# A fused fp32 transformer kernel on one core: the order of the thirty-four input-projection units is permuted

## The chip, the cores and the metric

The kernel runs on one core of a Trainium2 chip. The metric is the device time of one execution in microseconds (us); lower is better. The engines are called as the profile calls them: PE (TensorE, matmuls), DVE (VectorE), ACT (ScalarE), POOL (GpSimd), and SP, which here only issues transfers. Each runs its own list of instructions in order and waits on semaphores that the others raise.

## The reference

Two transformer blocks run one after the other on 512 tokens of width 1024, in fp32. What matters here is the middle of the first block:

```python
u = rmsnorm(h, mix_norm[l])
(fq, fk, fv, ff, dq, dk, dv, iq, ik, iw, mq, g) = jnp.split(u @ w_in[l], SPLIT_POINTS, axis=-1)
fq = rmsnorm(fq.reshape(B, S, FOX_HEADS, FOX_HEAD_DIM), fox_q_norm[l])      # fk alike
dq = rope(rmsnorm(dq.reshape(B, S, DSA_HEADS, DSA_HEAD_DIM), dsa_q_norm[l]), cos, sin)   # dk alike
iq = rope(iq.reshape(B, S, IDX_HEADS, IDX_DIM), cos_i, sin_i)               # ik alike
km, vm = jnp.split(rmsnorm(mem, mem_norm[l]) @ w_mem_kv[l], 2, axis=-1)
km = rmsnorm(km.reshape(B, M, MEM_HEADS, MEM_HEAD_DIM), mem_k_norm[l])
mq = rmsnorm(mq.reshape(B, S, MEM_HEADS, MEM_HEAD_DIM), mem_q_norm[l])
```

Before it stands a SwiGLU feed-forward layer. After it come three attentions (forget-gated "fox", top-k "dsa" whose keys an indexer picks, and one over 256 memory tokens), gates, an output projection, a second feed-forward layer, and then the second block.

## The kernel before

Activations lie transposed, with 128 features on the partitions and the tokens along the row. All weights form one stream of units of 128x1024 fp32, 512 KB each. SP loads unit u into a ring of four when unit u-4 is done. ACT casts it to a rounded high part (`high`), POOL subtracts to get the low part (`low_part`, line 436), and PE multiplies high by high, low by high and high by low (lines 503 to 505). One unit is 8 chunks by 3 matmuls, 24 in all, with 512 columns each. For `km` and `vm`, which project the 256 memory tokens, they have 256 columns. I call the former long units and the latter short ones.

The stage around the change is `stepped`, written once for each engine. It walks the table `IN_STEPS`, one unit of 128 output features a step. The kind of a unit decides what follows its matmuls. What follows is spread over the next steps:

- All kinds: DVE takes the result out of PSUM and multiplies by the token factor ("the take", line 1469). PE may start unit j only when unit j-3 is taken.
- `NORM` kinds (`fq fk dk dq mq km`), with a norm per attention group: ACT squares twice (1050, 1051), POOL splits off the low part of the square (481), and PE sums by group (`head_sums`, lines 636 and 637). PE does this sum for unit i right after the matmuls of unit i+1 and before those of unit i+2. For `km`, and for unit 1, `late_sums` puts it inside unit i+2, after the second of its eight chunks. Then ACT takes the root (1058), DVE the reciprocal (1521), and DVE scales (1502).
- `ROPE` kinds (`iq ik dq dk`): ACT copies rotated halves (1094), DVE does two products and a sum (1512 to 1514).
- `TURN` kinds (`fv vm ik dk`): PE transposes (674) after unit i+1, DVE copies out (1480, 1482).

On DVE the order within step j is fixed: take of unit j, copy-out of j-1, scaling of j-2, rope of j-3, reciprocal of j-1, then for j < 8 the low part of a memory chunk (1535).

```python
for i in ((0, 1) if j == 2 else (j - 1,)):
    kind, n = IN_STEPS[i], tokens(IN_STEPS[i])
    if kind in NORM and not late_sums(i):
        head_sums(i)
```

Some things are tied to step numbers and not to kinds: the norm of the memory tokens (steps 4 to 12), the forget gate (steps 9 to 17), and the copy of the shared keys `ki` and `kd` to the other 64 partitions by a transfer on ACT's queue (1104), four steps after the unit that makes them.

After the last unit PE runs the gate projection as filler: 14, 14 and 20 of its matmuls (line 723) in the three last steps. Then it waits for every take, norm, rope and transposition, and for both shared keys (`shared_keys`, 32), and begins the indexer's scores (line 768) with more gate matmuls between them.

Of the kernel before, what the change touches and what calls it, by code (L numbers as in the profile page):

```python
# [63 lines left out]

IN_STEPS = (["ik"] + ["fq"] * 4 + ["fk"] * 4 + ["iq", "mq", "iq", "dq"] + ["fv", "km", "vm", "dq"] * 3
            + ["fv", "km", "vm", "dk", "mq", "iq", "mq", "mq", "iq"])
GATES = 3 * DK


N_GU, N_DN, N_IN, N_BR, N_WO, N_IN2, N_WO2 = 2 * FC, FC, len(IN_STEPS) + GATES, 12, 8, 12, 8
U_GU1 = 0
# [73 lines left out]
def build(nc, T):  # L147
    ctx = ExitStack()
    with ctx:
# [163 lines left out]
        def upto_step(steps, kinds, j):  # L313

            return sum(k in kinds for k in steps[:j + 1])
# [4 lines left out]
        def tokens(kind):  # L320
            return MEM if kind in ("km", "vm") else S
# [36 lines left out]
        def gate_unit(g):  # L358
            return U_IN + len(IN_STEPS) + g

# [71 lines left out]
        def _(pool):  # L432
            def low_part(u, i=None):

                pool.wait_ge(high_done, u + 1 if i is None else i * RING + (u + 1))
                pool.tensor_tensor(wl[:, u % RING, :], raw[:, u % RING, :], wh[:, u % RING, :].bitcast(F32),  # L436
                                   ALU.subtract).then_inc(low_done, 1)
# [18 lines left out]
            def add_squares(name):  # L456

                for m in range(1, POOL_SQUARES):

                    pool.wait_ge(sem("input_square"), fed(name, m))  # L460
                    add_square(tiles[0][:, :], tiles[m][:, :])
# [6 lines left out]
            add_squares("mix")  # L468
            for j in range(2, len(IN_STEPS) + 2):
                low_part(U_IN + j)  # L470
# [5 lines left out]
                i = j - 2  # L476
                if IN_STEPS[i] in NORM:
                    k, n = upto_step(IN_STEPS, NORM, i), tokens(IN_STEPS[i])

# [19 lines left out]
        def _(pe):  # L499
# [122 lines left out]
            def late_sums(i):  # L622
                return i == 1 or (0 <= i < len(IN_STEPS) and IN_STEPS[i] == "km")

# [1332 lines left out]
```

## Time and profile before

| | |
|---|---|
| median of 3 runs | 1790.74 us (1790.39 to 1793.21) |
| time of the profiled execution | 1791.0 us |
| its span, first to last instruction | 1789.2 us |
| mean granted TensorE clock, as a share of full speed | 0.995 |
| PE busy | 1768.6 us, 99% of the span |
| DVE, ACT, POOL busy | 39%, 39%, 45% |
| the stage of the change, from the first take to the first score | 385.6 to 567.2 us |

A row of the timeline gives start, duration, engine, line, operation, result and operands, count, and in brackets how long the engine sat idle just before and what it waited for. Matmuls are pipelined, so that a row's duration (0.39 us for 512 columns) is longer than the distance to the next matmul. Distances between starts are therefore what counts on PE.

### The profile page before, as it was taken

Reading aid. Unit: us, or ns where it says so; the run is one execution under the profiler, and the core shown is the slowest. Engines: PE = TensorE matmul, PEld = TensorE weight load, DVE = VectorE, ACT = ScalarE, POOL = GpSimd, SP = SyncE. Lnnn points to the kernel's source line nnn. Section 1 sums busy time; section 2 is a strip of 40 time slices with the busy share of each in tenths; the row PEclk is TensorE's granted clock in tenths of the full one; section 3 lists DMA queues with packets and bytes.
Section 4 is the critical chain, followed back from the end, with each engine's and each line's share of the span. In section 5 each row is a group of like instructions: output and inputs, shape, how many; then the busy total and the mean of one; then the engine's idle time right before and its main releaser. Section 6 shows DMA issues by size and latency. Waiting matters only on the chain.

```text
span 1789.2 us, 23346 instructions
## 1 busy us (share of the span) xinstructions
PE 1768.6 (99%) x8472; PEld 1437.7 (80%) x8472; DVE 689.3 (39%) x1141; ACT 697.5 (39%) x1120; POOL 798.7 (45%) x368
## 2 busy tenths in 40 slices
PE   9999999999999999999999999999999999999997
PEld 7888888887887777787888888888866888888886
DVE  5222230077867874235352222200775522222002
ACT  5322231165554577784352223221425433222212
POOL 2444444466565433334454444444532444444442
PEclk9999999999999999999999999999999999999998
DMA  5322233322333221112322223322351222322231
GB/s 176 103 94 94 94 100 100 123 84 91 104 115 109 71 71 37 49 49 86 101 94 95 94 94 98 101 94 94 101 142 59 95 94 99 100 94 94 97 103 71
DMA packets 50495, 168.23 MB, mean 94 GB/s; under 512 B 6264, under 2 KB 7032, under 8 KB 50304
## 3 DMA queue, kind: packets, MB, share of 16 engines
q1 hardware_dynamic: 47088, 161.34, 27.5%
q10 hardware_dynamic: 3344, 6.05, 1.1%
q8 instruction: 40, 0.66, 0.2%
q14 instruction: 23, 0.19, 0.0%
HBM read 161.84 MB, written 2.11 MB: 92 GB/s over the span
## 4 chain that ended last, share of the span: by engine, by line
PE 94%; DVE 3%; issue 1%; ACT 1%; DMA 0%; POOL 0%; SPq 0%; DVEq 0%; ACTq 0%; POOLq 0%
PE bank L503 26%; PE bank L505 26%; PE bank L504 26%; PE bank L723 8%; PE bank L768 2%; PE bank L794 2%; PE bank L891 1%; PE bank L785 1%; DVE input_low L1371 0%; DVE tile L1388 0%; DVE bank L1521 0%; PE bank L582 0%; PE bank L774 0%; DVE mem_out_low L1660 0%; ACT tile L1203 0%
## 5 line engine op out<-in xcount | busy, mean ns | idle before, releaser
L436 POOL TENSOR_TENSOR weights_low<-raw_weights,weights_high 128x1024 fp32r<-128x1024 f32 x292 | 705.3, 2418 | 903.4 <-ACT weights_high L990 881.3
L503 PE MATMUL bank<-input_high,weights_high 128*128 128x512 f32 x1424 | 557.6, 392 | 0.4 <-DVE input_low L1371 0.3
L504 PE MATMUL bank<-input_high,weights_low 128*128 128x512 f32 x1424 | 554.5, 389 | 0.0
L505 PE MATMUL bank<-input_low,weights_high 128*128 128x512 f32 x1424 | 554.5, 389 | 0.0
L990 ACT CAST weights_high<-raw_weights 128x1024 fp32r<-128x1024 f32 x294 | 306.3, 1044 | 308.4 <-DMA raw_weights<-weights 290.3
L503 PEld LDWEIGHTS bank<-input_high,weights_high 128*128 128x128 f32 x1424 | 267.8, 188 | 58.9 <-issue 3.5
L505 PEld LDWEIGHTS bank<-input_low,weights_high 128*128 128x128 f32 x1424 | 267.5, 188 | 55.9
L504 PEld LDWEIGHTS bank<-input_high,weights_low 128*128 128x128 f32 x1424 | 267.7, 188 | 55.0 <-issue 0.2
L503 PE MATMUL bank<-hidden_high,weights_high 128*128 (+1 forms) x528 | 205.4, 389 | 0.0
L504 PE MATMUL bank<-hidden_high,weights_low 128*128 (+1 forms) x528 | 205.4, 389 | 0.0
L505 PE MATMUL bank<-hidden_low,weights_high 128*128 (+1 forms) x528 | 205.4, 389 | 0.0
L1441 DVE TENSOR_TENSOR tile<-bank,token_factor 128x512 f32<-128x512 f32 x66 | 45.6, 691 | 299.6 <-PE bank L505 299.6
L1122 ACT CAST hidden_high<-tile 128x512 f32 (+1 forms) x66 | 41.0, 621 | 302.8 <-DVE tile L1446 302.8
L1421 DVE SCALAR_TENSOR_TENSOR residual<-bank,residual 128x512 f32<-128x512 f32 x40 | 27.4, 686 | 259.1 <-PE bank L505 259.0
L503 PEld LDWEIGHTS bank<-hidden_high,weights_high 128*128 128x128 f32 x528 | 99.1, 188 | 20.6
L504 PEld LDWEIGHTS bank<-hidden_high,weights_low 128*128 128x128 f32 x528 | 99.1, 188 | 20.6
L505 PEld LDWEIGHTS bank<-hidden_low,weights_high 128*128 128x128 f32 x528 | 99.1, 188 | 20.5
L1117 ACT ACTIVATE tile<-tile 128x512 f32<-128x512 f32 x66 | 41.8, 633 | 180.6 <-DVE tile L1436 180.6
L1436 DVE TENSOR_TENSOR tile<-bank,token_factor 128x512 f32<-128x512 f32 x66 | 45.6, 691 | 135.6 <-PE bank L505 134.6
L723 PE MATMUL bank<-input_high,weights_high 128*128 128x512 f32 x192 | 77.9, 406 | 0.0
L723 PE MATMUL bank<-input_high,weights_low 128*128 128x512 f32 x192 | 76.8, 400 | 0.0
L723 PE MATMUL bank<-input_low,weights_high 128*128 128x512 f32 x192 | 76.7, 399 | 0.0
(243 smaller groups left out, 1843.2 us busy)
## 6 DMA issues: line engine op xcount, KB each, us to landing
raw_weights<-weights SPq DMA_DIRECT2D x294, 512.0 KB, 3.4
out_t<-out_t SPq DMA_DIRECT2D x8, 256.0 KB, 2.1
residual<-x_t SPq DMA_DIRECT2D x6, 256.0 KB, 5.9
glu_stacked<-glu_padded ACTq DMA_DIRECT2D x24, 64.0 KB, 3.9
glu_stacked<-glu_padded SPq DMA_DIRECT2D x24, 64.0 KB, 3.8
mem_in<-mem_t ACTq DMA_DIRECT2D x1, 1024.0 KB, 4.8
tile<-forget_sums ACTq DMA_DIRECT2D x4, 256.0 KB, 3.5
raw_weights<-weights SPq DMA_DIRECT2D x3, 256.0 KB, 5.7
```

Of the source, the lines that this page charges most:

```text
L436: pool.tensor_tensor(wl[:, u % RING, :], raw[:, u % RING, :], wh[:, u % RING, :].bitcast(F32), ALU.subtract).then_inc(low_done, 1)
L503: pe.matmul(out, wh[:, u % RING, w], rh, start=start, stop=False)
L504: pe.matmul(out, wl[:, u % RING, w], rh, start=False, stop=False)
L505: return pe.matmul(out, wh[:, u % RING, w], rl, start=False, stop=stop)
L723: mm = pe.matmul(bank[g % 2][:, :], (wl if part == 1 else wh)[:, u % RING, w], (xl if part == 2 else xh)[:, k, :], start=(k == 0 and part ...
L768: mm = pe.matmul(score_banks[n % 3][:, cols], left, right[:, cols], start=True, stop=not (kind == "fox" and last))
L794: mm = pe.matmul(heads_bank[lo:hi, q * P:(q + 1) * P], val, probs_t[n % 2][:, b * P:(b + 1) * P], start=(b == 0), stop=(b == ext // P - 1))
L990: act.copy(wh[:, u % RING, :], raw[:, u % RING, :]).then_inc(high_done, 1)
L1117: act.activation(tiles[c][:, :], tiles[c][:, :], ACT.Silu).then_inc(sem(f"{name}_silu"), 1)
L1122: act.copy(hh[:, f, :].rearrange("p a n -> p (a n)"), tiles[2 + c][:, :]).then_inc(sem(f"{name}_high"), 1)
L1436: dve.tensor_tensor(tiles[c][:, :], bank[2 * c][:, :], rstd[:, :], ALU.mult).then_inc(sem(f"{name}_gate"), 1)
L1441: dve.tensor_tensor(tiles[2 + c][:, :], bank[2 * c + 1][:, :], rstd[:, :], ALU.mult).then_inc(sem(f"{name}_banks"), 1)
```

## The change

Only the table is changed. The counts of each kind stay, and so do the rules that hang on a kind or on a step number. The host lays out the weight stream by the same table, so units and weights move together.

```diff
-IN_STEPS = (["ik"] + ["fq"] * 4 + ["fk"] * 4 + ["iq", "mq", "iq", "dq"] + ["fv", "km", "vm", "dq"] * 3
-            + ["fv", "km", "vm", "dk", "mq", "iq", "mq", "mq", "iq"])
+IN_STEPS = (["ik"] + ["fq", "fv", "fq", "iq"] * 2 + ["fk", "fv", "fk", "iq", "fk", "fv", "fk"]
+            + ["dq", "vm", "mq", "km", "iq", "dq", "vm", "mq", "km", "dq", "vm", "mq", "km", "dq", "km", "mq", "dk", "vm"])
```

Written out with their numbers, units 9 to 33 were: iq mq iq dq fv km vm dq fv km vm dq fv km vm dq fv km vm dk mq iq mq mq iq. They are now: fk fv fk iq fk fv fk (9 to 15), dq16 vm17 mq18 km19 iq20 dq21 vm22 mq23 km24 dq25 vm26 mq27 km28 dq29 km30 mq31 dk32 vm33.

First place: DVE near the start of the stage. `tile_107`, `108`, `109` and `112` are the four buffers that takes rotate through, and L1469 is a take. Before:

```order
L1502 SCALAR_TENSOR_TENSOR fox_q<-tile_109,vectors,bank 128x512
L1521 RECIPROCAL bank<-bank 128x512
L1535 SCALAR_TENSOR_TENSOR mem_low<-mem_in,vectors,mem_high 128x256
L1469 TENSOR_TENSOR tile_108<-bank,token_factor 128x512
L1502 SCALAR_TENSOR_TENSOR fox_q<-tile_112,vectors,bank 128x512
L1521 RECIPROCAL bank<-bank 128x512
L1535 SCALAR_TENSOR_TENSOR mem_low<-mem_in,vectors,mem_high 128x256
L1469 TENSOR_TENSOR tile_109<-bank,token_factor 128x512
```

Now:

```order
L1535 SCALAR_TENSOR_TENSOR mem_low<-mem_in,vectors,mem_high 128x256
L1469 TENSOR_TENSOR tile_107<-bank,token_factor 128x512
L1521 RECIPROCAL bank<-bank 128x512
L1535 SCALAR_TENSOR_TENSOR mem_low<-mem_in,vectors,mem_high 128x256
L1469 TENSOR_TENSOR tile_108<-bank,token_factor 128x512
L1502 SCALAR_TENSOR_TENSOR fox_q<-tile_112,vectors,bank 128x512
L1535 SCALAR_TENSOR_TENSOR mem_low<-mem_in,vectors,mem_high 128x256
L1469 TENSOR_TENSOR tile_109<-bank,token_factor 128x512
```

Every step had a reciprocal; now every other step has one.

Second place: DVE in the middle of the part with short units. `mem_token_factor` marks the take of a short unit. Before, from one reciprocal of a `dq` on:

```order
L1521 RECIPROCAL bank<-bank 128x512
L1469 TENSOR_TENSOR tile_109<-bank,mem_token_factor 128x256
L1480 COPY fox_v<-bank 128x4x128
L1502 SCALAR_TENSOR_TENSOR tile_107<-tile_107,vectors,bank 128x512
L1469 TENSOR_TENSOR tile_112<-bank,mem_token_factor 128x256
L1512 TENSOR_TENSOR tile_114<-tile_114,rope_sin 128x512
L1513 TENSOR_TENSOR tile_107<-tile_107,rope_cos 128x512
L1514 TENSOR_TENSOR dsa_q<-tile_107,tile_114 128x512
L1521 RECIPROCAL bank<-bank 128x256
L1469 TENSOR_TENSOR tile_107<-bank,token_factor 128x512
```

Now, from the reciprocal of dq25 to the take of dq29:

```order
L1521 RECIPROCAL bank<-bank 128x512
L1469 TENSOR_TENSOR tile_112<-bank,token_factor 128x512
L1480 COPY mem_v<-bank 128x2x128
L1502 SCALAR_TENSOR_TENSOR tile_108<-tile_108,vectors,bank 128x512
L1469 TENSOR_TENSOR tile_107<-bank,mem_token_factor 128x256
L1512 TENSOR_TENSOR tile_113<-tile_113,rope_sin 128x512
L1513 TENSOR_TENSOR tile_108<-tile_108,rope_cos 128x512
L1514 TENSOR_TENSOR dsa_q<-tile_108,tile_113 128x512
L1521 RECIPROCAL bank<-bank 128x512
L1469 TENSOR_TENSOR tile_108<-bank,token_factor 128x512
```

Between the rope of a `dq` and the take of the next `dq` stood the reciprocal of a `km`, 256 wide; now it is that of an `mq`, 512 wide.

Third place: ACT at the end of the stage. L1104 is the transfer that copies `dsa_k` (`kd`), L1030 takes the first gate out of PSUM, and L1185 is the first transfer of the next stage. Before:

```order
L1058 ACTIVATE bank<-bank,epsilons 128x512
L1094 COPY tile_114<-tile_109 32x512 x4
L1104 DMA dsa_k<-dsa_k 64x512
L1058 ACTIVATE bank<-bank,epsilons 128x512
L1094 COPY tile_113<-tile_108 32x512 x4
L990 CAST weights_high<-raw_weights 128x1024
L1030 COPY gates<-bank 128x512
L1185 DMA tile_107<-forget_sums 128x512
```

Now:

```order
L1058 ACTIVATE bank<-bank,epsilons 128x512 x2
L1094 COPY tile_113<-tile_107 32x512 x2
L990 CAST weights_high<-raw_weights 128x1024
L1030 COPY gates<-bank 128x512
L1104 DMA dsa_k<-dsa_k 64x512
L1185 DMA tile_107<-forget_sums 128x512
```

The copy of the shared key moved from step 32 of the stage to its last step, 36.

## Rows read from the trace of the kernel before

**Rows 1.** The page: busy time by engine.

```profile
PE 1768.6 (99%) x8472; PEld 1437.7 (80%) x8472; DVE 689.3 (39%) x1141; ACT 697.5 (39%) x1120; POOL 798.7 (45%) x368
```

**Rows 2.** Windows: stretch, length, busy us of PE, PEld, DVE, ACT, POOL, clock.

```profile
457.00:532.00 75.00, 75.00 (x435) 64.80 (x435) 56.87 (x56) 40.28 (x60) 46.24 (x25) 1.00 0.35 113
```

**Rows 3.** Waits of PE from 385 to 567 us: total, times, longest.

```profile
PE bank L636 <- POOL square_low L481: 1.7, 5, 0.4
```

**Rows 4.** Timeline of PE: four of the group sums behind `fq` and `fk` units.

```profile
395.09 0.39 PE L636 MATMUL bank<-square_high,ones_by_head_rounded 128*128 128x512 f32 x1
...
401.01 0.39 PE L636 MATMUL bank<-square_high,ones_by_head_rounded 128*128 128x512 f32 x1
...
413.89 0.50 PE L636 MATMUL bank<-square_high,ones_by_head_rounded 128*128 128x512 f32 x1 [0.36 <-POOL square_low L481]
...
433.55 0.50 PE L636 MATMUL bank<-square_high,ones_by_head_rounded 128*128 128x512 f32 x1 [0.37 <-POOL square_low L481]
```

**Rows 5.** Timelines of DVE, ACT and POOL in one such step, 410 to 417 us.

```profile
410.54 0.68 DVE L1469 TENSOR_TENSOR tile<-bank,token_factor 128x512 f32<-128x512 f32 x1
411.14 0.73 DVE L1502 SCALAR_TENSOR_TENSOR fox_q<-tile,vectors,bank 128x512 f32<-128x512 f32 x1
412.99 3.37 DVE L1521 RECIPROCAL bank<-bank 128x512 f32<-128x512 f32 x1 [1.11 <-ACT bank L1058]
416.26 0.92 DVE L1535 SCALAR_TENSOR_TENSOR mem_low<-mem_in,vectors,mem_high 128x256 fp32r<-128x256 f32 x1
...
411.25 0.63 ACT L1050 ACTIVATE tile<-tile 128x512 f32<-128x512 f32 x1 [3.19 <-DVE tile L1469]
...
412.31 0.64 ACT L1058 ACTIVATE bank<-bank,epsilons 128x512 f32<-128x512 f32 x1
...
412.55 1.29 POOL L481 TENSOR_TENSOR square_low<-tile,square_high 128x512 fp32r<-128x512 f32 x1 [2.21 <-ACT square_high L1051]
```

**Rows 6.** Timeline of PE around a short unit, 477 to 482 us.

```profile
477.53 0.39 PE L505 MATMUL bank<-input_low,weights_high 128*128 128x512 f32 x1
...
478.22 0.28 PE L503 MATMUL bank<-mem_high,weights_high 128*128 128x256 f32 x1
...
481.08 0.60 PE L674 MATMUL bank<-identity,tile 128*128 128x128 f32 x4
```

**Rows 7.** Timelines of DVE, ACT and POOL around the rope of a `dq`.

```profile
478.03 0.69 DVE L1469 TENSOR_TENSOR tile<-bank,token_factor 128x512 f32<-128x512 f32 x1 [2.37 <-PE bank L505]
...
486.67 0.69 DVE L1512 TENSOR_TENSOR tile<-tile,rope_sin 128x512 f32<-128x512 f32 x1 [1.58 <-ACT tile L1094]
...
487.99 2.77 DVE L1514 TENSOR_TENSOR dsa_q<-tile,tile 128x512 f32<-128x512 f32 x1
490.69 1.75 DVE L1521 RECIPROCAL bank<-bank 128x256 f32<-128x256 f32 x1
...
492.95 0.40 DVE L1480 COPY mem_v<-bank 128x256 f32<-128x256 f32 x1
...
484.13 2.51 ACT L1094 COPY tile<-tile 32x512 f32<-32x512 f32 x4 [0.55 <-issue]
...
487.79 2.43 POOL L436 TENSOR_TENSOR weights_low<-raw_weights,weights_high 128x1024 fp32r<-128x1024 f32 x1 [1.04 <-ACT weights_high L990]
```

**Rows 8.** The end of the stage: the key's transfer, the gate matmuls, the first score.

```profile
551.28 0.49 ACTq L1104 DMA_DIRECT2D dsa_k<-dsa_k  x1
...
dsa_k<-dsa_k ACTq DMA_DIRECT2D x1, 128.0 KB, 3.0
...
556.18 0.39 PE L723 MATMUL bank<-input_high,weights_high 128*128 128x512 f32 x1
...
567.17 0.71 PE L768 MATMUL bank<-idx_k,idx_q 64*128 64x128 f32 x8
```

**Rows 9.** Windows at the kernel's very end, columns as in rows 2.

```profile
1775.00:1780.00 5.00, 1.90 (x12) 1.87 (x13) 2.20 (x5) 2.18 (x3) 0.00 (x0) 0.89 0.00 0
1780.00:1783.00 3.00, 1.17 (x6) 0.88 (x5) 1.79 (x3) 0.00 (x0) 0.00 (x0) 0.50 0.06 21
```

## The prediction

> **What bounds the kernel now.** I read the page first. PE is busy 99% of the span and the other engines under half of it [rows 1], so time is saved or lost only where PE waits. Next came the windows. In the part of the stage with short units PE is busy for all of 75 us, at a granted clock of 1.00, while DVE is busy for 57 us and POOL for 46 us [rows 2]. That is cover, but not much of it. Third, PE's waits within the stage: there is one kind only, five times, for POOL's low part of a square [rows 3]. The timeline places it. The group sums behind the run of `fq` and `fk` units start 5.92 us apart while nothing is late (395.09 to 401.01), and from 401.01 to 433.55 there are five steps in 32.54 us [rows 4]. Five free steps would take 29.6 us, so the stalls cost 2.9 us.
>
> The cause is a ring through DVE and ACT [rows 5]. From the take (410.54) it is 0.71 us to the squares (411.25), 1.06 to the root (412.31), 0.68 to the reciprocal (412.99), 3.27 to the memory chunk (416.26), and its 0.92 less 0.08 of overlap to the next take: 6.56 us, more than PE's 5.92. It needs a reciprocal in every step.
>
> **What the change gives: the run is broken up.** Units with and without a norm alternate down to unit 15, so a ring has two steps, 11.8 us. All five stalls go: -2.9 us.
>
> **What it costs, 1: short units behind normed ones.** The sum of unit i is due when unit i+1 ends. Its work takes 0.50 us from the last matmul to the take (477.53 [rows 6] to 478.03 [rows 7]) and 3.35 us from take to sum (410.54 [rows 5] to 413.89 [rows 4]), 3.85 us together. A long unit i+1 covers it: 5.46 us (5.92 less 0.46 for two sum matmuls). A short one lasts 2.86 us (478.22 to 481.08 [rows 6]), with 0.23 for the last matmul before it: 3.09 us. The shortfall is 0.76 us, and 0.1 more because a matmul after a wait takes 0.50 us and not 0.39 [rows 4]. Before, only `km` had its squares beside a short unit, and its sum waits a unit longer. Now eight normed units have a short one behind them: dq16, mq18, dq21, mq23, dq25, mq27, dq29, dk32. What else stands there covers a part. For dq16 and dk32 that is another unit's sums (0.46), which leaves 0.4 each. Behind mq18, mq23 and mq27 it is a transposition of two blocks, about 0.25 by half of the row with four, which leaves 0.6. All matmuls of PE are queued behind such a wait.
>
> **2: DVE comes late to a `dq`.** I walk from the last matmul of mq23 (or mq27) to the sum of the next `dq`. Take starts after 0.50; take 0.60; copy-out of a `vm` 0.32 (0.40 less 0.08); scaling of the earlier `dq` 0.65; hand-over to ACT 0.11: 2.18 us. Rotation 2.51 and 0.03: 4.72. Three rope operations free of waits, 1.92 (486.67 to 487.99, and 0.60): 6.64. Then the reciprocal of the `mq`, now 3.27 where a `km` took 1.75: 9.91. Take to sum, 3.35: 13.26 us [rows 5, 7]. PE meanwhile has 0.23, the transposition 0.25, short unit 2.86, sums 0.46, long unit 5.46, the `km` sums 0.24, short unit 2.86: 12.36 us. The shortfall is 0.9, with two restarts 1.1 us, and the wait of the `mq` itself is in it.
>
> To this come waits between DVE and POOL. The third rope operation took 2.77 us instead of 0.68 while POOL made a low part, 487.79 to 490.22 [rows 7]: 2.1 us. In the new order I place POOL's work by the same rows. Its square starts 2.0 us after the take of the `mq` (410.54 to 412.55) and lasts 1.3, then a weight's low part of 2.4, until 5.7. The rope starts 4.2 us after the take and so waits 1.5 us. The next cast of ACT (1.0 us) follows the rotation, so POOL's next low part starts about when the second rope operation ends, and the third waits some 2.2 us. That is 3.7 us, 4.8 us a period. The bounds are 1.1 us with no wait and 7.4 us with all three at 2.1. There are two periods: 9.6 us.
>
> A rule bears on this. The Trainium skill, SBUF — State Buffer, section "Who interferes with whom", says that a DVE operation with both inputs in SBUF and a POOL operation exclude each other for the whole instruction. The row agrees with it in length. By the rule all three could be caught, and the sum below would be 5.2 us larger for the two periods; by the one wait that the row shows it would be 3.2 us smaller.
>
> **3: dq16 and dq21.** Before the take of dq16, DVE does the take of unit 15, a copy of 0.6, a scaling, the rope of iq12 and the forget sums' copy: 0.5+0.6+0.6+0.65+1.92+0.6 = 4.9 us after unit 15, due at 6.5. One port wait makes it 0.4 us late and two 2.6; I take 1.5, with the 0.4 above 1.9 us. For dq21 a long iq20 stands between. Its own shortfall is 0.86, and with two port waits 0.7 more; I take 1.3. mq18 costs 0.6.
>
> **4: the end.** `dk` moves from unit 28 to 32, and its transfer to ACT's last step. Before, it landed at 551.28+3.0 = 554.3, 12.9 us ahead of the first score at 567.17 [rows 8]. Now, from the last matmul of dk32: take done 1.1; a `km` scaling 0.4; rope of dq29 1.92; reciprocal of mq31 3.27; a short take 0.35, copy 0.32, scaling 0.65; reciprocal of dk32 3.27; copy 0.32, scaling 0.65: 12.25 us. Hand-over 0.11, rotation of half as many rows 1.26, rope 1.92, hand-over 0.11, transfer 3.0: 18.65 us. PE has 0.23+0.46+2.86+0.4+0.46, a transposition 0.4, 48 gate matmuls 10.99 (556.18 to 567.17 [rows 8]) and another 0.25: 16.0 us. The first score waits 2.7 us, and 2.1 more for each port wait among six rope operations. I take one: 4.8 us. dk32's own sum costs 0.4.
>
> **5: small things.** The norm of the memory tokens stays at steps 11 and 12, where a normed unit 11 and the rope of iq8 now stand in front of its reciprocal. With no port wait it is in time, with two it is 2.7 us late; 0.5. SP issues as many transfers, by units that end at the same rate; no two short units stand together now, so the ring is no tighter: 0. POOL does the same operations. A low part is due two units after the square ahead of it, at least 8.3 us later against 2.4: 0.
>
> **Sum.** -2.9 +0.5 +1.9 +0.6 +1.3 +9.6 +0.4 +4.8 = +16.2 us. The profiled execution took 1791.0 us (span 1789.2), so 1807.2. The median of the runs, 1790.74, lies 0.26 below it: 1807 us. Nothing later gives it back, since PE goes on at 99%.
>
> **Rivals.** A measurement of this kernel tells about 0.2%, 3.6 us, from no change.
>
> - Likeliest, 0.60: as summed, 1803 to 1811.
> - The port waits don't come (DVE and POOL slip past each other): periods 1.1 each, dq16 0.4, dq21 0.9, end 2.7, memory norm 0: -2.9+0.4+0.6+0.9+2.2+0.4+2.7 = +4.3, 1795. For it speaks that in the rope shown [rows 7] two of the three operations didn't wait. Against it, the two sequences above overlap by more than 1 us. 0.10.
> - They come everywhere, three a period and three at the end: +5.2 and +4.2, 1816. 0.08.
> - The clock falls in the waits. At the kernel's end PE was busy 1.90 of 5.00 us, and then the granted clock was 0.50, the 1.2 GHz level [rows 9]. If the wait before the first score does this and the low level lasts as long as the wait, 5 us, then PE loses 2.5 us, and as much in a period's wait: 1807+2.5 to 5, 1811. The Trainium skill, TensorE: Matmul & The Clock Gate, Part 1, says the clock falls after idling; no row here shows it in mid-kernel. 0.15.
> - Not slower: the chain from last matmul to sum shrinks under the short unit. It decides at 3.09 us; it is 3.85 in the run of `fq`, where ACT and POOL were free for it, and the 2.7 us at the end would have to be absent too. Then the -2.9 is left: 1788. 0.03.
> - It does nothing, since the losses equal 2.9: 1791. 0.04.
>
> Range 1799 to 1813: it leaves out the cases of 1788, 1791, 1795 and 1816 except for a part of their spread, some 0.2. Slower by over 0.2% (over 1794.4): 0.93. Within: 0.04. Faster: 0.03.
>
> **What would show it.** In the new trace the sums' waits (L636 for POOL) vanish before unit 15 and come back behind dq16, mq18, dq21, dq25 and dq29, with the largest, 3 to 5 us, behind dq25 and dq29. Ropes of dq21 and dq25 have one or two rows over 1.5 us. The first L768 waits some 5 us for ACT's transfer. The prediction is wrong if DVE reaches the takes of dq25 and dq29 within 0.6 us of their last matmuls, or the key lands before the gate matmuls end.

## The result and the profile after

The changed kernel takes 1809.01 us (median of 4 runs, 1807.45 to 1809.68), the kernel before 1790.57 us in the same job (1789.56 to 1793.21). The ratio is 1.0101, with a 95% interval of 1.0086 to 1.0116, so it is slower by 18.4 us. Three executions that came out far longer than all others (4518.27 and 2210.44 us of the kernel before, 10159.95 us of run e9) stand in no ratio and no range below. The profiled execution took 1809.26 us with a span of 1807.5, against 1791.0 and 1789.2 before.

The page's busy times, which answer to [rows 1], and the first of its rows of slices. PE's own work has not changed in number; the span grew by 18 us and PE's busy time by 5.

```profile
span 1807.5 us, 23345 instructions
PE 1773.4 (98%) x8472; PEld 1440.8 (80%) x8472; DVE 696.7 (39%) x1141; ACT 697.9 (39%) x1120; POOL 803.4 (44%) x368
PE   9999999999988999999999999999999999999997
```

PE is now below nine tenths in the twelfth and thirteenth slice, 497 to 587 us. The waits of PE from 385 to 590 us (total, times, longest), which answer to [rows 3]:

```profile
PE bank L636 <- POOL square_low L481: 9.0, 8, 3.3
PE bank L768 <- DMA dsa_k<-dsa_k: 4.7, 1, 4.7
PE bank L697 <- DVE token_root L1378: 0.5, 1, 0.5
```

Before, there were five waits for the low part of a square, 1.7 us together. Now there are eight, and two kinds that did not exist. PE's timeline (start, length, engine, line; in brackets the idle time before and who ended it) says where:

```profile
448.91 0.71 PE L697 MATMUL bank<-identity,token_root 128*128 128x128 f32 x4 [0.49 <-DVE token_root L1378]
479.87 0.50 PE L636 MATMUL bank<-square_high,ones_by_head_rounded 128*128 128x512 f32 x1 [1.69 <-POOL square_low L481]
489.85 0.50 PE L636 MATMUL bank<-square_high,ones_rounded 128*128 128x512 f32 x1 [0.69 <-POOL square_low L481]
505.08 0.50 PE L636 MATMUL bank<-square_high,ones_by_head_rounded 128*128 128x512 f32 x1 [0.53 <-POOL square_low L481]
514.89 0.50 PE L636 MATMUL bank<-square_high,ones_rounded 128*128 128x512 f32 x1 [0.49 <-POOL square_low L481]
527.44 0.78 PE L636 MATMUL bank<-square_high,ones_by_head_rounded 128*128 128x512 f32 x1 [3.28 <-POOL square_low L481]
538.67 0.50 PE L636 MATMUL bank<-square_high,ones_rounded 128*128 128x512 f32 x1 [0.32 <-POOL square_low L481]
549.74 0.50 PE L636 MATMUL bank<-square_high,ones_by_head_rounded 128*128 128x512 f32 x1 [1.75 <-POOL square_low L481]
565.24 0.50 PE L636 MATMUL bank<-square_high,ones_by_head_rounded 128*128 128x512 f32 x1 [0.28 <-POOL square_low L481]
582.43 1.23 PE L768 MATMUL bank<-idx_k,idx_q 64*128 64x128 f32 x8 [4.69 <-DMA dsa_k<-dsa_k]
589.00 0.71 PE L768 MATMUL bank<-idx_k,idx_q 64*128 64x128 f32 x8
```

In this order they are the norm of the memory tokens, the sums of dq16, mq18, dq21, mq23, dq25, mq27, dq29 and dk32, and the first and second score. The first score started at 567.17 before [rows 8], so 15.3 of the 18.3 us are there at 582.43. Between the first and the second score another 3.0 come: 6.57 us now, 3.59 before. Look at the lengths in two of the rows: the sum behind the 3.28 us wait took 0.78 us and not 0.50, and the score behind the 4.69 us wait 1.23 and not 0.71. That is the clock. The windows have the columns of [rows 2] (after the clock come the share of DMA and its GB/s):

```profile
524.00:527.40 3.40, 0.16 (x2) 0.00 (x0) 2.50 (x4) 2.44 (x4) 1.28 (x2) 1.00 0.50 157
527.40:530.00 2.60, 2.56 (x6) 2.07 (x7) 2.09 (x4) 1.31 (x2) 2.60 (x2) 0.52 0.02 6
530.00:533.00 3.00, 3.00 (x12) 2.41 (x12) 2.75 (x1) 0.31 (x1) 2.07 (x1) 0.85 0.00 0
577.00:582.40 5.40, 0.74 (x4) 0.28 (x2) 4.09 (x3) 0.43 (x1) 4.05 (x2) 0.97 0.44 142
582.40:585.00 2.60, 2.57 (x11) 2.12 (x12) 0.47 (x1) 2.09 (x4) 1.20 (x1) 0.50 0.88 292
585.00:588.00 3.00, 3.00 (x8) 2.31 (x7) 2.83 (x2) 0.00 (x0) 2.58 (x2) 0.50 0.18 66
```

During the waits the granted clock is 1.00 or near it. Right behind them PE is busy for the whole of the window, and the clock is 0.50, the 1.2 GHz level. These two waits are thus paid twice, by their length and by the clock behind them. Behind dq25 the matmuls are 0.43 us apart instead of 0.23 until 530.6, behind the first score until 588.5.

The period from mq23 to dq25 on DVE, the engine that is late there. L1512 to L1514 are a rope's three operations, L1469 is a take, L1521 a reciprocal:

```profile
511.41 0.69 DVE L1469 TENSOR_TENSOR tile<-bank,token_factor 128x512 f32<-128x512 f32 x1 [1.08 <-PE bank L505]
...
513.61 1.78 DVE L1513 TENSOR_TENSOR tile<-tile,rope_cos 128x512 f32<-128x512 f32 x1
515.42 2.77 DVE L1514 TENSOR_TENSOR idx_q<-tile,tile 128x512 f32<-128x512 f32 x1
518.23 0.42 DVE L1469 TENSOR_TENSOR tile<-bank,mem_token_factor 128x256 f32<-128x256 f32 x1
518.57 0.68 DVE L1512 TENSOR_TENSOR tile<-tile,rope_sin 128x512 f32<-128x512 f32 x1
519.16 0.69 DVE L1513 TENSOR_TENSOR tile<-tile,rope_cos 128x512 f32<-128x512 f32 x1
519.89 1.12 DVE L1514 TENSOR_TENSOR dsa_q<-tile,tile 128x512 f32<-128x512 f32 x1
520.93 3.35 DVE L1521 RECIPROCAL bank<-bank 128x512 f32<-128x512 f32 x1
524.19 0.67 DVE L1469 TENSOR_TENSOR tile<-bank,token_factor 128x512 f32<-128x512 f32 x1
```

and on POOL beside it:

```profile
513.37 1.46 POOL L481 TENSOR_TENSOR square_low<-tile,square_high 128x512 fp32r<-128x512 f32 x1 [3.61 <-ACT square_high L1051]
514.80 2.85 POOL L436 TENSOR_TENSOR weights_low<-raw_weights,weights_high 128x1024 fp32r<-128x1024 f32 x1
```

POOL is done with the low part of mq23's square at 514.83, and the cosine product of iq20's rope ends 0.56 us later (515.39). POOL is done with the low part of the weights at 517.65, and the rope's sum ends 0.54 us later (518.19). So both operations waited for the end of POOL's. Against 0.69 and 0.68 us free these are 1.1 and 2.1 us. The next rope loses 0.4 more: 3.6 us, and the reciprocal of mq23 is behind all of it.

The operations are back to back from 511.41 on, up to the take of dq25 at 524.19. PE waits for the square of that take.

### The profile page after: what moved, and what is told of

It reads as the page before. It is cut to its first block, busy times and chain, and to the rows that moved or that the text cites. A ratio compares the mean times of both kernels' runs of the same rounds, so it can differ in the third digit from the quotient of the medians.

```text
span 1807.5 us, 23345 instructions
## 1 busy us (share of the span) xinstructions
PE 1773.4 (98%) x8472; PEld 1440.8 (80%) x8472; DVE 696.7 (39%) x1141; ACT 697.9 (39%) x1120; POOL 803.4 (44%) x368
## 4 chain that ended last, share of the span: by engine, by line
PE 91%; DVE 5%; ACT 1%; issue 1%; POOL 0%; DMA 0%; DVEq 0%; SPq 0%; ACTq 0%
PE bank L503 25%; PE bank L504 25%; PE bank L505 25%; PE bank L723 7%; PE bank L768 2%; PE bank L794 2%; PE bank L891 1%; DVE bank L1521 1%; PE bank L785 1%; DVE input_low L1371 1%; DVE tile L1469 1%; DVE tile L1388 0%; DVE tile L1513 0%; POOL square_low L481 0%; PE bank L582 0%
```

## Experiments

All are edits of the changed kernel unless said otherwise; e8 is an edit of e4, and e9 of the kernel before. The ratios are to the kernel before in the same job, whose median was 1790.57 to 1790.91 each time. My theory was that the time is the sum of the late sums and the late key, with port waits and clock falls on top; each run takes one of these away or puts one of them alone.

**e1: PE is kept busy in the last wait.** Ahead of the first score PE makes 22 matmuls that nobody reads, into an idle bank. The extra work, with a wait for that bank in front of it, is the only difference.

```diff
+            pe.wait_ge(sem("forget_out"), 1)
+            for _ in range(22):
+                pe.matmul(bank[6][:, :], xh[:, 0, 0:P], xh[:, 0, :], start=True, stop=True)
```

> Changed kernel with 22 extra matmuls of 512 columns (5.0 us at 0.2275 us each, results never read) between the last gate filler and the wait for the shared key, so that PE isn't idle there. Theory A, the clock fell because PE idled for 4.7 us: the granted clock stays 1.00 after the first score, the stretch from the first score to the second goes from 6.57 back to about 3.6 us, and the time falls by 2.6 to 3.0 us, to 1806.2; the first score itself does not move. Rival: the slow matmuls after the first score come from the transfers that land then; they stay, and the time stays at 1809.

Measured: 1806.27 us (1804.71 to 1806.9, 5 runs), ratio 1.0084 (1.0071 to 1.0097). The traced execution is the fastest of the five. PE's timeline:

```profile
527.54 0.50 PE L636 MATMUL bank<-square_high,ones_by_head_rounded 128*128 128x512 f32 x1 [3.26 <-POOL square_low L481]
537.14 0.50 PE L636 MATMUL bank<-square_high,ones_rounded 128*128 128x512 f32 x1 [0.31 <-POOL square_low L481]
581.02 0.71 PE L768 MATMUL bank<-idx_k,idx_q 64*128 64x128 f32 x8
584.61 0.72 PE L768 MATMUL bank<-idx_k,idx_q 64*128 64x128 f32 x8
```

The second score follows the first by 3.59 us, as before the change, with the key as late as ever. Work in the wait saves the 3.0 us of the clock and nothing of the wait. The trace holds a second finding. Behind the wait of dq25, of the same length here (3.26 us against 3.28), the clock did not fall this time:

```profile
527.40:530.00 2.60, 2.46 (x11) 2.04 (x12) 2.58 (x4) 1.66 (x3) 2.60 (x3) 1.00 0.03 8
```

From that sum to mq27's it is 9.60 us here and 11.23 in the changed kernel, so the fall at dq25 costs 1.6 us there, and does not come in every execution. That is why the traced execution is 4.5 us below the changed kernel's, and the median only 2.7.

**e2: the shared key comes earlier.** `iq` at unit 20 and `dk` at unit 32 change places.

```diff
-            + [..., "mq", "km", "iq", "dq", "vm", ..., "mq", "dk", "vm"])
+            + [..., "mq", "km", "dk", "dq", "vm", ..., "mq", "iq", "vm"])
```

> Changed kernel with units iq20 and dk32 exchanged. Theory A: the key lands long before the first score, so the 4.7 us wait and the clock's fall (3.0 us) vanish; iq32's rope, 2.5 us of rotation but no reciprocal and no transfer, leaves up to 2 us of wait. The waits behind dq25 and dq29 (3.3 and 1.8 us) stay. About 1803, range 1801 to 1805. Rival B, the end wait only collects a lateness of DVE that would show elsewhere: time within 2 us of 1809.

Measured: 1803.08 us (1798.85 to 1803.3, 6 runs), ratio 1.0059 (1.0047 to 1.0072). Waits of PE, 385 to 590 us:

```profile
PE bank L636 <- POOL square_low L481: 8.4, 6, 3.5
PE bank L674 <- DVE tile L1469: 1.7, 1, 1.7
PE bank L697 <- DVE token_root L1378: 0.5, 1, 0.5
```

The wait for the key is gone, and the two first scores are 3.60 us apart (579.95 and 583.55). The gain is 5.9 us and not the 7.7 of wait and clock together: PE now waits 1.73 us for the take of iq32 at 571.84, and the low clock behind dq25 lasted longer (12.28 us from its sum to mq27's). Two of the six executions took 1798.85 and 1800.22 us, at a mean clock of 0.997 and 0.996 instead of 0.994. That fits executions in which the clock did not fall, but none of them was traced. The waits of dq25 and dq29 stayed (3.46 and 1.74).

**e3: the rope's sum no longer meets POOL.** From unit 13 on the rope's sine product goes to an idle PSUM bank, so the rope's last operation, the sum, has one of its inputs in PSUM.

```diff
-  dve.tensor_tensor(halves[k % 2][0:m, :], halves[k % 2][0:m, :], sin[0:m, :], ALU.mult)
+  turned = bank[6][0:m, :] if i >= 13 else halves[k % 2][0:m, :]
+  dve.tensor_tensor(turned, halves[k % 2][0:m, :], sin[0:m, :], ALU.mult)
...
-  dve.tensor_tensor(out, t, halves[k % 2][0:m, :], ALU.add).then_inc(sem("in_roped"), 1)
+  dve.tensor_tensor(out, t, turned, ALU.add).then_inc(sem("in_roped"), 1)
```

> Changed kernel in which, from unit 13 on, the rope's sine product is written to PSUM bank 6 and the rope's sum reads it there, so that the third rope operation has one input in SBUF and not two. Theory A, waits between DVE and POOL for two SBUF inputs are part of DVE's lateness: no L1514 row over 1.1 us after unit 13, the wait behind dq29 or dq25 falls by 1 to 2 us, the first score's wait falls from 4.7 to about 2.4 us and with it most of the clock's fall: 1801 to 1804. Rival, the long L1514 rows only follow POOL's load and DVE is late by its own work: the waits behind dq25, dq29 and at the end stay within 0.5 us, 1808 to 1809.

Measured: 1801.81 us (1800.48 to 1803.23, 6 runs), ratio 1.006 (1.0047 to 1.0072). The rope's sum, 480 to 580 us (times, then shortest, median and longest in ns), in the changed kernel:

```profile
L1514 DVE TENSOR_TENSOR dsa_q<-tile,tile x4: 1117/1120/1666, 493.3 to 564.1; 128x512 f32<-128x512 f32 x4
L1514 DVE TENSOR_TENSOR idx_q<-tile,tile x1: 2774/2774/2774, 515.4 to 515.4; 128x512 f32<-128x512 f32 x1
L1514 DVE TENSOR_TENSOR dsa_k<-tile,tile x1: 2727/2727/2727, 577.2 to 577.2; 64x512 f32<-64x512 f32 x1
```

and in e3:

```profile
L1515 DVE TENSOR_TENSOR dsa_q<-tile,bank x4: 687/688/690, 493.5 to 562.9; 128x512 f32<-128x512 f32 x4
L1515 DVE TENSOR_TENSOR idx_q<-tile,bank x1: 686/686/686, 515.6 to 515.6; 128x512 f32<-128x512 f32 x1
L1515 DVE TENSOR_TENSOR dsa_k<-tile,bank x1: 680/680/680, 575.0 to 575.0; 64x512 f32<-64x512 f32 x1
```

Not one sum waits any more, with the same POOL work. dq25's wait went from 3.28 to 2.34 us, dq29's from 1.75 to 1.31, the first score's from 4.69 to 1.69: 4.4 us. The run gained 7.2. In the traced executions the second score came 5.6 us earlier, of which 1.4 are clock: it stood 5.18 us behind the first, against 6.57. The Trainium skill, SBUF — State Buffer, section "Who interferes with whom", says that a DVE instruction with at most one SBUF input, outside the two-port perf modes, doesn't contend with GpSimd; 2.77 us against 0.69 agrees.

The rope's two products still have both inputs in SBUF, and some of them still wait. In e3, ahead of the take of dq25:

```profile
513.82 1.77 DVE L1514 TENSOR_TENSOR tile<-tile,rope_cos 128x512 f32<-128x512 f32 x1
516.69 1.72 DVE L1513 TENSOR_TENSOR bank<-tile,rope_sin 128x512 f32<-128x512 f32 x1
```

With a third one of 1.23 us they lose 2.6 us, where the ropes of the changed kernel lose 3.6 at this place. The difference is what PE's wait fell by (0.94). The same holds for dq29 (0.45 and 0.44) and for the first score (3.0 and 3.0). So a port wait on this path reaches PE in full. The waits that are left don't show that something else made them, since 2.6 us of port waits are left too; a kernel with none at all was not run.

**e4: the last eighteen units in another order.** The first sixteen stay as in the changed kernel.

```diff
-            + ["dq", "vm", "mq", "km", "iq", "dq", "vm", "mq", "km", "dq", "vm", "mq", "km", "dq", "km", "mq", "dk", "vm"])
+            + ["iq", "vm", "km", "km", "km", "mq", "dk", "dq", "vm", "vm", "mq", "dq", "km", "mq", "dq", "dq", "mq", "vm"])
```

> The changed kernel's first sixteen units, then the other eighteen regrouped so that dq16-dk-like units mostly have a long unit or another short one behind them: iq vm km km km mq dk dq vm vm mq dq km mq dq dq mq vm. Theory A: the alternation gives 2.9 less 0.5 us, and nothing of the tail's loss is left but some tenths: first score at 565 to 566 us (567.2 before), time 1788 to 1790. Rival C, alternating units cost something of their own (streams of weights, fox_v copies): 1793 or more.

Measured: 1790.48 us (1788.81 to 1791.37, 11 runs), ratio 0.9994 (0.9986 to 1.0003). The waits:

```profile
PE bank L768 <- DVE causal_mask_rounded L1638: 1.2, 1, 1.2
PE bank L697 <- DVE token_root L1378: 0.5, 1, 0.5
```

With the first sixteen as they are, another order of the last eighteen takes away all of the 18.4 us. But it is no gain over the kernel before either, though the five stalls of the run are gone here. The first score starts at 567.38, 0.2 us later than in the kernel before. Of the 2.9 us the two waits took 1.7 back and their restarts 0.2; the sums at 527.12 and 554.28 came 3.6 us after the sum ahead (523.51 and 550.65), where one that is not late behind one short unit comes after 3.3 (554.29 to 557.61 in e6), which makes 0.6. The rest, some 0.6 us, I can't place.

**e5: the run of the kernel before, with the last eighteen units of the changed one.**

```diff
-IN_STEPS = (["ik"] + ["fq", "fv", "fq", "iq"] * 2 + ["fk", "fv", "fk", "iq", "fk", "fv", "fk"]
+IN_STEPS = (["ik"] + ["fq"] * 4 + ["fk"] * 4 + ["iq", "fv", "iq", "fv", "iq", "fv", "fv"]
```

> The other half of the change alone: the run of four fq and four fk as before, then iq fv iq fv iq fv fv, then the changed kernel's eighteen last units. Theory A: the five stalls in the run (2.9 us) are back, the memory norm's wait (0.5) is gone, dq16's wait falls from 1.7 to about 0.5 us, and everything from mq18 on stays, with both falls of the clock: 1809 to 1811. Rival, the loss in the tail is a lateness carried over from the alternating part: the waits behind dq21, dq25 and dq29 shrink by 1 us or more each, 1806 or less.

Measured: 1808.8 us (1807.97 to 1809.88, 4 runs), ratio 1.0101 (1.0085 to 1.0116). The waits:

```profile
PE bank L636 <- POOL square_low L481: 9.2, 13, 3.3
PE bank L768 <- DMA dsa_k<-dsa_k: 4.7, 1, 4.7
```

The five stalls of the run are back (0.24 to 0.37 each), and eight from dq16 on stand beside them. The time is the changed kernel's nonetheless. The order of the first sixteen units had cost elsewhere most of what it gained: dq16's wait is 0.49 here instead of 1.69, mq18's 0.32 instead of 0.69, and the 0.49 at the norm of the memory tokens is gone. Together that is 2.1 us, against 2.9; the first score is 2.1 us later here (584.51), of which 1.2 come from a longer stretch at the low clock behind dq25 (12.39 us to the next sum, against 11.23).

**e6: no low part of the squares.** POOL doesn't make it, and the second sum matmul multiplies the high part again. The computation is changed: the sum of squares comes out about twice as large. PE's work stays the same.

```diff
-  pool.tensor_tensor(sq_low[k % 2][:, 0:n], sq_in[k % 2][:, 0:n], sq_high[k % 2][:, 0:n].bitcast(F32),
-                     ALU.subtract).then_inc(sem("in_square_low"), 1)
...
-  pe.wait_ge(sem("in_square_low"), k)
+  pe.wait_ge(sem("in_square_high"), k)
...
-  pe.matmul(norm_banks[k % 2][:, 0:n], group, sq_low[k % 2][:, 0:n], start=False, stop=True
+  pe.matmul(norm_banks[k % 2][:, 0:n], group, sq_high[k % 2][:, 0:n], start=False, stop=True
```

> Changed kernel without POOL's low part of the squares; the second of the two sum matmuls takes the high part again, so PE's work is the same (the norms are not the reference's). The chain from a unit's last matmul to its sum is 1.3 us shorter, 2.5 us. Theory A, a short unit of 3.1 us covers 2.5: the waits behind mq18, mq23, mq27 and dk32 vanish (2.3 us of PE time), those behind dq21, dq25, dq29 fall by up to 1.3 us each, so that the clock falls at most once: 1799 to 1803. Rival, these waits come from DVE's lateness only: the small ones behind the mq units stay, 1806 or more.

Measured: 1802.99 us (1801.72 to 1803.14, 4 runs), ratio 1.0068 (1.0052 to 1.0083). The waits (its lines stand six above those of the changed kernel):

```profile
PE bank L762 <- DMA dsa_k<-dsa_k: 4.9, 1, 4.9
PE bank L630 <- ACT square_high L1045: 3.5, 2, 1.8
PE bank L668 <- DVE tile L1463: 1.3, 1, 1.3
```

The other six waits for a square are gone: without the 1.3 us of POOL the chain is shorter than a short unit. Those of dq25 and dq29 remain with 1.84 and 1.63 us, now for ACT's square: there DVE's take is late, whatever follows it. They fell by 1.4 and by only 0.1 us, since POOL's work lies otherwise now: in both periods the rope's sum waits for a weights' low part (2.78 us, at 513.11 and 534.66). A new wait of 1.31 us for a take stands at 563.36. The clock fell twice, and not at most once as I had expected: behind the wait of 1.84 us the matmuls are 0.43 us apart until 524.5, and again behind the first score.

**e7: half a reciprocal for `mq`.** It is made for 256 of the 512 tokens; for the others the root stays as it is, so that their norm is left out.

```diff
-  root_k = norm_banks[k % 2][:, 0:n]
+  root_k = norm_banks[k % 2][:, 0:MEM if IN_STEPS[i] == "mq" else n]
```

> Changed kernel in which the reciprocal of an mq unit covers 256 of 512 tokens, as long as a km's (1.75 and not 3.27 us; the norm of half of the tokens is not the reference's). Theory A: the reciprocal of the mq stands between the rope of one dq and the take of the next, so the waits behind dq25 and dq29 and the first score's wait fall by 1.5 us each where nothing else catches up, the small waits behind the mq units stay: 1802 to 1805. Rival: PE's wait is set by ACT or POOL, and nothing moves, 1808 to 1809.

Measured: 1804.02 us (1803.74 to 1804.17, 4 runs), ratio 1.0075 (1.006 to 1.0091). PE's timeline has

```profile
525.88 0.50 PE L636 MATMUL bank<-square_high,ones_by_head_rounded 128*128 128x512 f32 x1 [1.66 <-POOL square_low L481]
545.15 0.50 PE L636 MATMUL bank<-square_high,ones_by_head_rounded 128*128 128x512 f32 x1 [0.33 <-POOL square_low L481]
```

The two waits shrank by 1.62 and 1.42 us, the reciprocal by 1.6 us (3.35 against 1.75). The other waits on squares stayed within 0.1 us. So the wide reciprocal ahead of the take of a `dq` is on the path that sets both waits. The first score's wait stayed too (4.75 us), and I had expected it to fall by 1.5. The key's transfer did go out 6.2 us earlier than in the changed kernel (573.79), while PE came to its wait only 4.7 us earlier, but the transfer took 3.8 us to land instead of 2.2. Why is open. Behind the 1.66 us the clock stayed at 1.00, which gives the other 1.6 us up to the first score (577.81).

**e8 and e9: e3's edit where no rope is on the path.** e8 is e4 with the sine product in PSUM, e9 is the kernel before with it.

> The regrouped tail together with the rope's sum read from PSUM. With the regrouped tail alone the first score waited 1.2 us for DVE. Theory A: DVE comes to the end earlier, that wait goes or halves, first score at 566 us: 1789 to 1790, 1 us below the kernel before. Rival: DVE's end is set by the last units' own chain and nothing moves, 1790.5.

Measured: 1791.11 us (1789.11 to 1792.72, 11 runs), ratio 1.0001 (0.9992 to 1.001). The wait before the first score stayed, 1.19 us against 1.22, so port waits of the ropes' sums were not what made it.

> The kernel before with the rope's sum read from PSUM from unit 13 on, the edit that took 7 us off the changed kernel. Theory A: where every normed unit has a long unit behind it, DVE's lateness is covered, so nothing moves: within 1 us of the kernel before. Rival: the edit is a gain of its own by less port contention, 2 us or more off.

Measured: 1790.81 us (median of 12 runs, 11 of them at 1789.02 to 1793.28), ratio 1.0003 (0.9994 to 1.0012). The same five stalls, the first score at 567.25. DVE's busy time from 385 to 567 us fell from 140.84 to 134.35 us and nothing came of it: what is worth 7 us in one order is worth nothing in the other.

**e10: an order that spreads both kinds of work**, which on paper leaves neither a run of `fq` and `fk` nor a late `dq` or key.

```diff
+IN_STEPS = ["ik", "fk", "fv", "fk", "fv", "fq", "dq", "mq", "iq", "fv", "dq", "fq", "iq", "mq", "iq", "vm", "km",
+            "dq", "mq", "fv", "vm", "km", "dq", "vm", "km", "fk", "mq", "km", "vm", "fq", "fk", "dk", "fq", "iq"]
```

> Another order of the same units: no run of normed units while the memory chunks are made, no long normed unit with a single short one behind it and DVE late, dk at 31 with two long units behind it: ik fk fv fk fv fq dq mq iq fv dq fq iq mq iq vm km dq mq fv vm km dq vm km fk mq km vm fq fk dk fq iq. Theory A: the 2.9 us of stalls go and less than 0.5 us comes back: first score at 564 to 565 us, 1787.5 to 1788.5. Rival: something comes back at the end or behind a short pair as with the regrouped tail, 1790 to 1791.

Measured: 1790.34 us (1788.86 to 1792.62, 11 runs), ratio 0.9999 (0.999 to 1.0008). The expected gain of two to three us did not come. PE waits 0.6 us at the norm of the memory tokens, 0.3 for one square and 0.5 before the first score, which is all that is left. The first score starts at 566.77, 0.4 us earlier than in the kernel before. Such a gain is below what can be seen: runs of the kernel before itself lie between 1789.0 and 1794.0 us, with a mean clock of 0.997 at the fast end and 0.994 at the slow end. No version beats the kernel before.

## Why the prediction was right, and where not

The direction, the places of the waits and the time (1807 predicted, 1809.0 measured, within the range) were right. The terms, measured in PE's timeline as the distance from the matmul before the wait to the one behind it, less the same distance without a wait, with 0.1 us for the slow first matmul behind it:

| term | predicted us | measured us |
|---|---|---|
| stalls in the run | -2.9 | -2.9 |
| norm of the memory tokens | 0.5 | 0.7 |
| dq16 | 1.9 | 1.9 |
| mq18 | 0.6 | 1.0 |
| dq21 | 1.3 | 0.8 |
| mq23 and dq25 | 4.8 | 4.3 |
| mq27 and dq29 | 4.8 | 2.6 |
| dk32 | 0.4 | 0.5 |
| key, up to the first score | 4.8 | 4.8 |
| clock behind dq25 | 0 | 1.6 |
| clock behind the first score | 0 | 3.0 |
| sum | 16.2 | 18.3 |

**The run is broken up: shown.** Up to unit 15 no sum waits, and sums that are two steps apart start 11.4 to 12.3 us apart. The forecast had the lateness of dq16 and of the memory norm as terms of their own. What it did not say is that they are the price of the same alternation: e5 gives back 2.1 us there and loses 2.9 in the run, and its median is the changed kernel's within 0.2 us.

**Short units behind normed ones: shown.** The waits are at the forecast places, and all but those of dq25 and dq29 go with the 1.3 us low part (e6). dq25's take came 3.5 us after its last matmul (520.68 to 524.19) and dq29's 2.0 (544.50 to 546.49), where 0.6 was the bound for being wrong. But dq29's wait of 1.75 us was not among the 3 to 5 us that I expected for it.

**DVE comes late to a `dq`: the mechanism was right, and its pieces are shown** by e7 (reciprocal), e6 (the take is late) and e3 (port waits). One term is mis-sized, the 3.7 us of port waits taken for both periods. Before dq25 they were 3.6, but not where I had placed them: the walk left out the rope of iq20, which stands in that period too and itself costs nothing, since ACT rotates dq21 meanwhile. It carried 3.2 of the 3.6 us. Before dq29, the period which the walk did describe, two rope operations waited 1.0 and 0.4 us (DVE's rows at 539.81 and 542.18). POOL has the low part of km28's square ahead of the next low part of the weights in its list; it got that square from ACT only at 541.5, and so the weights' low part of 2.84 us began at 542.71, when the rope was all but over. So this period cost 2.6 us and not 4.8. I had worked out one sequence and applied it twice.

**The ropes of dq21 and dq25 with one or two rows over 1.5 us:** dq21's has none (1.12 at most), dq25's has one (1.73); the long ones are iq20's.

**The end: right, with two errors that cancel.** Two rope operations waited for POOL, 1.0 and 2.1 us, where I took one of 2.1; the transfer landed 2.2 us after its issue, where I took 3.0.

**The clock: the step that failed.** The likeliest case let PE wait up to 4.8 us at an unchanged clock and put the fall into a rival at 0.15, since no row of mid-kernel showed one. It fell behind the two longest waits. The two falls cost 4.6 us together, and the other terms together came out 2.5 us below their forecast (-2.7 in the two periods, 0.2 elsewhere). That these errors nearly cancel is luck, and it is why the total came out near. The rival "the clock falls in the waits" had it by mechanism and was also nearest in time after the likeliest: 2.5 for the end, measured 3.0; for a period up to 2.5, measured 1.6. e1 shows it for the first score: with PE busy in the wait, the scores are 3.59 us apart again.

The opposite rivals are out: the port waits came, not in every rope operation, and the chain did not shrink below a short unit.

## What to carry to other kernels

When units of unequal length share a chain of helpers, look at what stands *behind* a unit with a long chain: there the time must be as long as the chain, and alternation can spoil this as easily as it breaks up a run. Walk each period with its own neighbours, since the same pattern with one more operation in it meets another engine's work at another moment. On a TensorE that is otherwise never idle, a wait can cost its own length and the clock behind it as well (here 1.6 and 3.0 us behind 3.3 and 4.7), and work put into a long one pays (e1). Whether several short waits cost less than one long one was not tested; the clock fell behind waits of 1.69 and 1.84 us too.

## What the runs showed of the hardware

- The clock can fall behind a short wait in mid-kernel, and whether it does is not decided by the length of the wait alone. Behind 3.28 us at dq25 it was 0.52, behind 3.26 us at the same place in e1 1.00. It fell behind 1.84 us in e6 (0.52 at 521 to 523.6). In e3 it was down for a part of the stretch behind 2.34 us (0.72 at 526.7 to 530) and behind 1.69 us (0.65 at 580 to 584). It stayed at 1.00 behind 1.66 us in e7 and behind 1.73 us in e2 (571.8 to 578). The Trainium skill, TensorE: Matmul & The Clock Gate, Part 1, says of the warm-up at a kernel's start that the moment of the change varies from run to run; that one execution fell at dq25 and the other did not fits this in mid-kernel. Of the changed kernel's four runs three had a mean clock of 0.992 and one, the fastest at 1807.45 us, 0.994. That fits an execution with one fall fewer, but it was not traced.
- The fall shows only behind the wait: at 577 to 582.4, with PE busy for 0.74 of 5.40 us, the granted clock was 0.97, and at 582.4 to 588, with PE busy throughout, 0.50. In e3 it came later still: behind the 2.34 us wait the matmuls were 0.23 us apart until 528.2 and then 0.43 until 531.6. The price is half of the low stretch after work has come back: some 3 us of it behind dq25 (1.6 us), some 6 behind the first score (3.0 us).
- A rope operation that met a POOL operation ended 0.54 to 0.56 us behind POOL's end, whichever of the two kinds it was. The seven cases in DVE's and POOL's rows from 511 to 580 us, rope against POOL: 515.39 and 514.83, 518.19 and 517.65, 521.01 and 520.45, 541.54 and 540.99, 543.30 and 542.75, 565.74 and 565.19, 579.96 and 579.41. What is lost is thus about what is left of POOL's operation, here 0.4 to 2.1 us. It goes the other way too: the weights' low parts that POOL had next in the first, third, fifth and sixth case took 2.83 to 2.85 us, and not 2.4. The sum of 2.8 us stands in the rope of every `iq` from 422 us on (422.77, 446.00, 473.32 and 515.42), while those of the four `dq` took 1.1 to 1.7 us.
